# Three moves in a hybrid retention and attention step: first loads to other queues, the second tile's x ahead of five gate weights, gates ahead of four roundings

## The reference

```python
h = rmsnorm(x, norm_g)
rq, rk, rv, rg, aq, ak, av, ag, iq, ik, iw = split(h @ w_in)
# branch A: chunked retention, 4 heads of 128
ro = rmsnorm(retention(rope(rq), rope(rk), rv, state), ret_gn_g) * silu(rg)
# branch B: an indexer picks the top 256 keys of each query, then softmax attention, 8 heads of 64
ao = attend(top_k(index(rope(iq), rope(ik), iw)), rope(aq), rope(ak), av) * silu(ag)
y = rmsnorm(x + concat(ro, ao) @ w_out, final_g)
```

## Time and profile before

| | |
|---|---|
| three timed runs | 885.86 us median, 882.8 to 886.93 |
| the profiled execution's own time | 887.83 us |
| its span, first to last instruction | 886.3 us |
| busy share of the span | PE 88%, DVE 54%, ACT 38%, POOL 19% |
| granted TensorE clock, mean | 0.952 |
| the chain that ended last, by engine | PE 58%, DVE 17%, issue 8%, ACT 7%, DMA 5%, POOL 3% |

### The profile page before, as it was taken

How to read it: one execution, slowest core, us unless ns; L and a number is a source line. 1 busy time by engine, 2 the same in 40 slices (tenths; PEclk the granted TensorE clock), 3 DMA queues, 4 the chain that set the end, 5 groups by cost and what they waited for, 6 DMA issues and landing times.

```text
span 886.3 us, 12246 instructions
## 1 busy us (share of the span) xinstructions
PE 783.0 (88%) x4141; PEld 659.8 (74%) x4141; DVE 481.8 (54%) x1189; ACT 334.5 (38%) x755; POOL 168.7 (19%) x362
## 2 busy tenths in 40 slices
PE   1988978897989999979895999999996999999993
PEld 1777867786877878858783888888775888888872
DVE  3643576778777877779842433333365533232234
ACT  3654455566657466565562111111135200000010
POOL 0333223122222202110103222222221010111111
PEclk9998979899999979889996999999998999999997
DMA  7522112111203001103525212121456534333331
GB/s 207 195 79 80 36 31 85 61 55 57 59 14 137 9 12 61 29 13 98 170 81 164 90 65 66 65 65 65 138 157 176 158 102 118 118 118 118 118 95 36
DMA packets 36111, 79.80 MB, mean 90 GB/s; under 512 B 12688, under 2 KB 14112, under 8 KB 34784
## 3 DMA queue, kind: packets, MB, share of 16 engines
q1 hardware_dynamic: 28720, 59.03, 21.6%
q0 software_dynamic: 6464, 19.36, 7.1%
q10 hardware_dynamic: 880, 0.83, 0.4%
HBM read 58.67 MB, written 20.53 MB: 89 GB/s over the span
## 4 chain that ended last, share of the span: by engine, by line
PE 58%; DVE 17%; issue 8%; ACT 7%; DMA 5%; POOL 3%; ACTq 0%; DVEq 0%; SPq 0%; POOLq 0%
PE bank L853 40%; PE bank L1005 4%; DMA xT<-turned_x 3%; DVE probs L1688 3%; PE bank L994 3%; PE bank L872 2%; DVE work L1543 2%; PE bank L885 2%; DVE w_lo L1434 2%; DVE idx L1524 1%; ACT pT L1246 1%; DMA stage<-in_w_out 1%; DMA rope_t<-in_rope_att 1%; ACT probs L1235 1%; PE bank L988 1%
## 5 line engine op out<-in xcount | busy, mean ns | idle before, releaser
L853 PE MATMUL bank<-w_hi,xT 128*128 128x512 f32 (+1 forms) x1072 | 351.9, 397 | 24.3 <-DMA xT<-turned_x 11.2
L853 PEld LDWEIGHTS bank<-w_hi,xT 128*128 128x128 f32 x1072 | 204.8, 194 | 70.2 <-issue 14.7
L853 PE MATMUL bank<-w_lo,xT 128*128 128x512 f32 (+1 forms) x536 | 209.9, 392 | 0.0
L853 PEld LDWEIGHTS bank<-w_lo,xT 128*128 128x128 f32 x536 | 104.2, 194 | 17.6
L1005 PE MATMUL bank<-v_sb,pT 128*128 128x64 f32 x648 | 92.9, 285 | 5.6 <-ACT pT L1246 5.1
L1005 PEld LDWEIGHTS bank<-v_sb,pT 128*128 128x128 f32 x648 | 87.0, 205 | 11.5 <-ACT pT L1246 10.5
L853 PE MATMUL bank<-w_hi,mT 128*128 128x512 f32 x256 | 81.8, 395 | 0.0
L994 PE MATMUL bank<-ident,probs 128*128 128x128 f32 x324 | 56.8, 288 | 21.9 <-ACT probs L1235 21.9
L1246 ACT COPY pT<-bank 128x512 f32<-128x512 f32 (+3 forms) x104 | 49.3, 488 | 69.8 <-PE bank L994 69.1
L1235 ACT ACTIVATE probs<-probs,low 128x128 f32<-128x128 f32 (+8 forms) x68 | 54.4, 801 | 39.6 <-DVE low L1688 39.5
L994 PEld LDWEIGHTS bank<-ident,probs 128*128 128x128 f32 x324 | 40.6, 152 | 30.8 <-ACT probs L1235 28.6
(11 more groups left out here) (204 smaller groups left out, 1189.1 us busy)
## 6 DMA issues: line engine op xcount, KB each, us to landing
xT<-turned_x SPq DMA_DIRECT2D x34, 512.0 KB, 4.2
stage<-in_w_in SPq DMA_DIRECT2D x40, 256.0 KB, 3.2
turned_x<-xT SPq DMA_DIRECT2D x9, 1024.0 KB, 5.4
y_row<-in_x_prompt SPq DMA_DIRECT2D x16, 256.0 KB, 5.2
stage<-in_w_out SPq DMA_DIRECT2D x16, 256.0 KB, 3.9
out<-y_row POOLq DMA_DIRECT2D x16, 256.0 KB, 2.4
xin<-in_x_prompt SPq DMA_DIRECT2D x14, 256.0 KB, 3.7
early<-in_w_in SPq DMA_DIRECT2D x3, 1024.0 KB, 7.1
```

What stands on the lines that cost most here:

```text
L853: mm = pe.matmul(out, (lo if which == 2 else hi)[:, k, :], (w_lo if which == 1 else w_hi)[slot][:, k, 0:width], start=(i == 0), stop=(i == ...
```

## The change

The first x goes out on SP ahead of the weights of `iq`. ACT's queue keeps the identity, `cst` and `g_in`, in this order. `rope_t` and `fold_t` go to POOL's queue under a semaphore of their own, `tables_in`, for which POOL waits before its first rotation and PE before the `fold` matmuls; the other waits become 48. On SP the x of retention tile 1 is issued after three of the `rg` weights instead of six, and the last five follow it. On ACT and DVE the first four of `wo0` are rounded and split after `gates(0)` and `mix(0)`, with the other four, not ahead of the square and the norm of SAMPLE.

```diff
@@ SP @@
+            for half in range(2):
+                sp.dma_start(xin[half * DEC:(half + 1) * DEC, :], xp[half * DEC:(half + 1) * DEC, :])\
+                  .then_inc(x_in, 16)
             load_early("iq")
...
-            for i in range(item_no["rv", 0], item_no["rg", 2 * STAGES]):
+            for i in range(item_no["rv", 0], item_no["rg", STAGES]):
                 load(i)
             load_turned("R", 1)
-            for k in range(2 * STAGES, KD):
+            for k in range(STAGES, KD):
                 load(item_no["rg", k])
...
@@ PE, ahead of the fold matmuls @@
+                        pe.wait_ge(tables_in, 32)
-            pe.wait_ge(const_in, 80)
+            pe.wait_ge(const_in, 48)
...
@@ ACT @@
-            for half in range(2):
-                act.dma_start(xin[half * DEC:(half + 1) * DEC, :], xp[half * DEC:(half + 1) * DEC, :])\
-                   .then_inc(x_in, 16)
-            act.dma_start(g_in[:], norm_g).then_inc(const_in, 16)
             act.dma_start(ident[:], identity).then_inc(const_in, 16)
             act.dma_start(cst[:], small).then_inc(const_in, 16)
-            act.dma_start(fold_t[:], fold).then_inc(const_in, 16)
-            act.dma_start(rope_t[:], rope_att.rearrange("p (t n) -> p t n", n=2 * ROT)).then_inc(const_in, 16)
+            act.dma_start(g_in[:], norm_g).then_inc(const_in, 16)
-            act.wait_ge(const_in, 80)
+            act.wait_ge(const_in, 48)
...
-            for k in range(4):
-                round_w("wo0", k)
             square(SAMPLE)
             gates(0)
-            for k in range(4, KD):
+            for k in range(KD):
                 round_w("wo0", k)
...
@@ DVE @@
-            for k in range(4):
-                split_w("wo0", k)
             retain(SAMPLE, state_s, DEC)
...
             mix(0)
-            for k in range(4, KD):
+            for k in range(KD):
                 split_w("wo0", k)
...
@@ POOL @@
-            pool.wait_ge(const_in, 80)
+            pool.dma_start(rope_t[:], rope_att.rearrange("p (t n) -> p t n", n=2 * ROT)).then_inc(tables_in, 16)
+            pool.dma_start(fold_t[:], fold).then_inc(tables_in, 16)
+            pool.wait_ge(const_in, 48)
...
             power(power_no("A", 0), 1)
+            pool.wait_ge(tables_in, 32)
             rotate_iq(0)
```

More of the change, by code:

```diff
@@ L386, in hybrid_stream_step @@
         const_in = sem("const_in")
+        tables_in = sem("tables_in")
         x_in = sem("x_in")
@@ L1715, in _ @@
             dve.memset(ones8[:], 1.0).then_inc(ones_ready, 1)
-            dve.wait_ge(const_in, 80)
+            dve.wait_ge(const_in, 48)
             dve.wait_ge(ones_ready, 1)
```

## The result

The change made the kernel faster, about as forecast: 875.25 us (median of five runs, 872.66 to 880.29) against 886.33 for the kernel before in the same measurement (five runs, 882.8 to 889.29), a ratio of 0.9864 with a 95% interval of 0.9833 to 0.9895. That is 11.1 us less between the medians, where 14.7 were forecast. A second measurement of the same kernel, among the experiments, gave 877.25 against 887.79, 10.5 us less between the medians, with a ratio of 0.9905 (0.9876 to 0.9933). The ratios here are worked out from all the runs of both kernels; they are not the quotients of the two medians.

The account below looks back on a forecast made before the run. PE was taken as the bound, nearly gapless except for waits at the front, second retention tile and gates. Gains of 4.7 + 4.5 + 5.5 = 14.7 us gave a median of 871 from 885.86, range 865.5 to 878.

Parts of the forecast that it names:

- A, front: Kernel start: with x first and `rope_t` off ACT's wait, PE's first product starts at 16.0, not 20.74; 4.7 us.
- B, x ahead: Second retention tile: PE's 10.58 us wait for x goes and a shorter one for `kd_row` follows; 4.5 us gained.
- C, gates: Gates: PE's 6.77 us wait for ACT's silu goes, but output weights are then late; 5.5 us gained.
- late next: Front: ACT's rounding next waits for `iq` 4 and 5 in the 1 MB transfer, expected at 13.4.
- The bound of 3.6: Front: gain of only 3.6 us if the 1 MB transfer slips by the full 1.19, to 14.6.
- I scale the excess by 0.6 and put the operation at 482: Second retention tile: POOL's 12.04 us gap exceeds 7.2 by 4.8, taken as traffic; less traffic puts `kd_row`'s result at 483.0.
- The cold charge, 2.5: Second retention tile: PE's 6.4 us wait for `kd_row` lets the clock fall again, charged at 2.1 to 2.9, say 2.5.
- Rival 2: Second retention tile: POOL's gap is fixed, perhaps by three table loads; 2.1 us gained there, 873.5 in all; chance 0.2.
- Rival 3: Second retention tile: POOL's gap shrinks to 7.2 and the clock holds; 9.9 us gained there, 866 in all; chance 0.17.
- I take 4.6: 695.9 for the last split: Output weights: each of five stage-buffer cycles takes 4.6 us instead of 5.9, so `wo1` 7 is split at 695.9.
- The wait forecast late in y1: Second output product: its last three matmuls wait for the split of `wo1` until 695.9, ending at 696.8.
- Rival 1: Output weights: their cycle stays at 5.9 us, so moving the gates gives nothing; 877 in all; chance 0.13.

Follow-up runs that it names:

- the two kernels with copies: The changed kernel plus one, or six, 1 MB DRAM-to-DRAM copies on SP behind the sixth gate weight: 879.3 us (one), 887.36 us (six).
- the early operation: The changed kernel plus one small unread POOL operation behind the load of `fg_t`: 868.94 us against 887.74 before, ratio 0.9791.
- the other runs: The changed kernel with POOL's three table loads moved behind `kd_row` (gap 8.69; 874.0 us), and with six 1 MB copies added (gap 13.31; 887.36 us).
- the kernel with y1 on stand-in weights: The changed kernel with tile 0's y1 made with y0's weights, the wait for the last `wo1` moved to the next tile: 875.52 us against 887.74 before.
- the one with early copies: The changed kernel with tile 0's turned mixed rows copied ahead of the last two `wo0` on ACT and DVE: 875.17 us against 887.74 before.
- The fourth buffer: The changed kernel with a fourth stage buffer for the output weights, in the memory of `dec_t`: 871.85 us against 886.97 before, ratio 0.983.

## Why the prediction came out as it did

| term, us | forecast | landmarks of the profiled pair | alone, by the ratio (interval) | alone, between medians |
|---|---|---|---|---|
| A, front | 4.7 | 5.9 | 3.8 (1.9 to 5.8) | 4.8 |
| B, x ahead | 4.5 | 3.1 | 1.4 (-0.7 to 3.6) | 2.6 |
| C, gates | 5.5 | 1.6 (2.5 as a mean of traces) | 4.0 (1.9 to 6.1) | 4.1 |
| sum | 14.7 | 10.6 | 9.2; the whole 12.1 and 8.4 | 11.4; the whole 11.1 and 10.5 |

The mechanisms held, all three: each stall named was the one that bound, and each went. The sum was 3 to 6 us too large, for B and C. The medians of 875.25 and 877.25 lie in the range of 865.5 to 878, near its slow end; the median forecast, 871, was 4 to 6 us too fast.

**A was right, step by step.** What was named as late next, `iq` 4 and 5 in the 1 MB transfer, is what ACT waits for; it was there at 12.70, not 13.4, and the product started at 15.43, not 16.0. The bound of 3.6, in which the issues of x delay that transfer, did not come about.

**B had its mechanism right and two sizes off.** PE's wait for x went and one for `kd_row` took its place, 7.03 us where 6.4 were forecast, with the clock down. The step "I scale the excess by 0.6 and put the operation at 482" asked for a gap of about 10.0, 2 us less; measured were 10.91 in the profile and 10.4 as the mean of six traces with B done, against 11.5 over the three with it undone, so 1.1 us less. The 12.04 that the forecast scaled was the longest of those three (11.03 and 11.28 in the others). The premise held: the two kernels with copies have the longest gaps, and the traffic in the gap did fall to about 0.6, from 2.6 to 1.6 MB (212 GB/s over 12.04 us, 145 over 10.91). But the excess over 7.2 fell only from 4.8 to 3.7, so scaling it with the bytes was wrong. The cold charge, 2.5, measured 2.9. Rival 2, with the gap tied to the three table loads, falls with the early operation: they stand where they stood, and the gap is gone. A gap of fixed length is ruled out by the 8.69 and 13.31 us of the other runs, though by its time alone B can't be told from that rival's 2.1. Rival 3, a gap of 7.2 and a warm clock, did not come by itself; the early operation brings 11.5 us against before by the same landmarks, by paying where nobody waits.

The Trainium skill (GPSIMD Engine Reference, section 2.1, Instruction dispatch) has the first call of a freshly loaded kernel pay about 6 us without a visible instruction. The early operation agrees in kind: the first ordinary call pays (7.43 here), and the next ones don't. The figure agrees with the gaps ahead of the reduction itself (5.62 to 6.21 us, six times in after) and is below every gap on the way back, 7.0 to 13.3; that transfers stretch those is shown by the runs here alone.

**C failed in the step "I take 4.6: 695.9 for the last split", with a cold charge of nothing behind it.** The gates came as forecast: PE waits 0.77 us there, where none was forecast. Set in the time of before (7.4 us later, by the last scores), the first split of `wo0` came at 674.1, not 672.9; five cycles of the buffers took 24.6 us, 4.9 each and the first 6.2; y0 started at 686.7 and not 684.3, and the last split was there at 698.7 and not 695.9. The loads of the output weights meet those of `retained`, `mixed` and `state` there, and land in 4.6 us (median, DMAs issued 645 to 672). The second half of the miss is the clock: the forecast charged it at B but not at C, where PE waited 3.2 us and y0 and y1 together took 14.0 us instead of 11.2. The wait forecast late in y1 hardly appeared, since the slow y0 covered it; the kernel with y1 on stand-in weights shows it (no gain), and the one with early copies turns the low clock back into that wait. Rival 1, a cycle that stays at 5.9, was nearer by the gain of the profiled pair, but the cycle itself, 4.9, is nearer the forecast, and the timed runs put C between the two. The base of 5.9 was also the longest of three: the two other traces with C undone have 5.4. So the last split comes no more than 0.5 us earlier with C, counted from the last scores (36.9 as the mean of six traces, 37.3 over the three without); y0 starts 4.6 us earlier, and from there to the turned rows it takes 2.1 longer.

The fourth buffer shows what C could have been: with the cycle no longer binding, the stretch from the last scores to the turned rows of tile 1 falls by 5.7 us more.

## What to carry to other kernels

When a stall is removed, price what is late next with the rows of that very stage. Here both of the next waits were named and both were longer than taken, and behind each the clock was low, which cost 2.9 us behind the wait of 7.03 and about as much behind that of 3.16 (1.4 to 2.9 behind waits of 2.5 to 3.8 at that place, in seven traces). Look at what a helper engine does the first time after a special operation: one dummy operation in its idle time was worth 8.3 us in the traces, more than any of the three moves. And where weights go through a ring of buffers, count buffers before moving work around them.

## What was not expected of the hardware

POOL's first ordinary operation after its reduction waits, with nothing in the trace that it waits for: 7.0 to 7.9 us in five places of after's attention phase, at DMA shares from 0.09 (7.71) to 0.37 (7.17), and 8.69 to 13.31 ahead of `kd_row`, at shares from 0.46 to 1.06. The gap runs on beside transfers and is longest with the most of them, but the share alone doesn't order it. What it fetches or waits for stays open; the trace has no record of it.

The granted clock decides some stretches by what looks like a toss: 32 matmuls at the end of the kernel took 7.7 or 9.3 us behind the same PE wait of 1.85 us, eight of SAMPLE's `q` 2.1 or 3.5, in kernels that don't differ there. What decides isn't shown. Two executions can differ by 3 us from this alone, as much as a whole term of the sum; a single pair of profiles can't size such a term.
